# One gate unit moved from the state-space stage to the second attention, and a wait on copies put behind the products that don't read them

## The reference, cut to what matters

```python
proj = h @ w_in                      # the last 3 * 1024 columns are gate_logits
o_mla = causal_block_attention(q_mla, k_mla, v_mla)
o_fox = causal_block_attention(q_fox, k_fox, v_fox, cum_log_f)
o_s5 = s5_branch(u, ...)
gates = sigmoid(gate_logits.reshape(bsz, seq, 3, 1024))
merged = einsum('bsnd,bsnd->bsd', gates, projected)
x = x + merged @ w_out
x = x + conv_gated_ffn(rms_norm(x), ...)
```

## Time and profile before

| what | value |
|---|---|
| median of 3 runs | 1455.21 us (1454.87 to 1455.35) |
| the profiled execution: its own time | 1453.84 us |
| its span, first to last instruction | 1451.8 us |
| mean granted clock of PE, as a share of full speed | 0.998 |
| PE busy | 1430.5 us (99%), 7067 matmuls |
| DVE / ACT / POOL busy | 985.6 / 664.0 / 157.7 us |
| fox attention, about | 170 to 327 us |
| second attention, its first scores to its last values | 377.4 to 528.2 us |
| state-space stage up to its output products | 532.5 to 630.4 us |

### The profile page before, as it was taken

The page is one execution under the profiler, slowest core; times in us unless marked ns, Lnnn a source line. Parts: engine busy times, 40 slices in busy tenths (PEclk is TensorE's granted clock), DMA queues, the critical chain, the costliest instruction groups (busy, mean ns, idle before and its releaser), DMA issues.

```text
span 1451.8 us, 19018 instructions
## 1 busy us (share of the span) xinstructions
PE 1430.5 (99%) x7067; PEld 1203.3 (83%) x7067; DVE 985.6 (68%) x1430; ACT 664.0 (46%) x1074; POOL 157.7 (11%) x163
## 2 busy tenths in 40 slices
PE   8999999999999999999999999999999999999998
PEld 6999988888788888887888888888888888888887
DVE  5213556656866557839927688877778786678886
ACT  6231455645445542136513455555555555544332
POOL 1001620112361112013201000000000000000000
PEclk9999999999999999999999999999999999999999
DMA  7202021140121133337552222222222222990222
GB/s 267 63 0 95 26 73 45 51 160 28 46 60 52 37 88 95 75 127 245 187 219 70 88 73 88 87 87 73 75 86 87 88 87 84 325 388 30 94 73 80
DMA packets 130406, 148.94 MB, mean 103 GB/s; under 512 B 11338, under 2 KB 95229, under 8 KB 130045
## 3 DMA queue, kind: packets, MB, share of 16 engines
q1 hardware_dynamic: 130128, 147.68, 30.8%
q10 hardware_dynamic: 189, 0.08, 0.0%
HBM read 110.83 MB, written 36.31 MB: 101 GB/s over the span
## 4 chain that ended last, share of the span: by engine, by line
PE 89%; DVE 4%; ACT 2%; DMA 2%; issue 1%; SPq 1%; POOL 1%; ACTq 0%; DVEq 0%
PE ps L2195 29%; PE ps L673 13%; PE ps L2502 5%; PE ps L2504 5%; PE ps L2503 5%; PE ps L2593 4%; PE ps L370 3%; PE ps L371 3%; PE ps L372 3%; PE ps L862 2%; PE ps L3075 2%; PE ps L3073 2%; PE ps L3074 2%; PE ps L841 2%; PE ps L1504 2%; DMA scr_gate<-plain_arena 1%
## 5 line engine op out<-in xcount | busy, mean ns | idle before, releaser
L2195 PE MATMUL ps<-split_arena 128*128 128x512 f32 x1320 | 306.8, 390 | 0.0
L673 PE MATMUL ps<-split_arena 128*128 128x512 f32 x1152 | 291.1, 400 | 2.1 <-ACT plain_arena L708 2.1
L2195 PEld LDWEIGHTS ps<-split_arena 128*128 128x128 f32 x1320 | 247.6, 188 | 51.4 <-issue 0.3
L673 PEld LDWEIGHTS ps<-split_arena 128*128 128x128 f32 x1152 | 209.1, 189 | 42.8 <-issue 3.6
L2378 ACT ACTIVATE down_ops<-down_all 128x1024 fp32r<-128x1024 f32 x77 | 81.6, 1061 | 115.5 <-PE ps L2504 115.4
L2195 PE MATMUL ps<-up_b,split_arena 128*128 128x512 f32 x528 | 126.5, 389 | 0.0
L2397 DVE TENSOR_TENSOR down_ops<-down_all,down_ops 128x1024 fp32r<-128x1024 f32 x77 | 94.0, 1222 | 46.4 <-ACT down_ops L2378 46.3
L2502 PE MATMUL ps<-down_ops 128*128 128x512 f32 x308 | 120.0, 390 | 0.5 <-DVE down_ops L2397 0.5
L2503 PE MATMUL ps<-down_ops 128*128 128x512 f32 x308 | 120.0, 389 | 0.0
L2504 PE MATMUL ps<-down_ops 128*128 128x512 f32 x308 | 119.9, 389 | 0.0
L2195 PEld LDWEIGHTS ps<-up_b,split_arena 128*128 128x128 f32 x528 | 99.2, 188 | 20.5
(11 more groups left out here) (406 smaller groups left out, 2465.1 us busy)
## 6 DMA issues: line engine op xcount, KB each, us to landing
plain_arena<-in_w_in SPq DMA_DIRECT2D x24, 512.0 KB, 4.2
scr_gate<-plain_arena SPq DMA_DIRECT2D x48, 256.0 KB, 2.0
plain_arena<-scr_gate SPq DMA_DIRECT2D x24, 512.0 KB, 4.6
plain_arena<-in_w_up SPq DMA_DIRECT2D x22, 512.0 KB, 5.3
up_raw<-in_w_up SPq DMA_DIRECT2D x22, 512.0 KB, 4.9
scr_act<-plain_arena SPq DMA_DIRECT2D x22, 512.0 KB, 2.6
down_all<-scr_act SPq DMA_DIRECT2D x18, 512.0 KB, 9.4
down_all<-in_w_down SPq DMA_DIRECT2D x18, 512.0 KB, 10.2
```

What stands on the lines that cost most here:

```text
L673: mm = nc.tensor.matmul(m.ps[:, self.banks[half], :], w[:, k, :], src[:, k, h * BANK:(h + 1) * BANK], start=(j == 0), stop=(j == self.PER_ ...
L2195: mm = nc.tensor.matmul(o, self.w[j][w][:, k, :], self.h[j][k][h], start=(j in self.OPENS and k == 0 and n == 0), stop=(k == self.HK - 1 a ...
```

## The change

The number of units in the second attention goes from 6 to 7 and that of the s5 stage from 8 to 7; in the s5 stage 8 halves rather than 9 stand before the turning of w, so each of the stage's two long fills is 24 matmuls shorter. `MLA_FILL` takes the 48 matmuls: 24 more in head 0, 12 more in head 1, 12 more in head 2, none in head 3. Inside the heads they also change places. The second edit moves PE's wait for the copies of the turned w from ahead of the taps' products to behind them. SP's program text is not touched; its loops follow the constants.

```diff
--- before.py
+++ after.py
@@ -721,8 +721,8 @@
 
 
 
-FOX_FIRST, FOX_ATT, MLA_FIRST, MLA_PREP, MLA_ATT, S5_UNITS = 1, 6, 1, 2, 6, 8
-S5_FIRST_HALVES = 9
+FOX_FIRST, FOX_ATT, MLA_FIRST, MLA_PREP, MLA_ATT, S5_UNITS = 1, 6, 1, 2, 7, 7
+S5_FIRST_HALVES = 8
 FOX_UNITS = FOX_FIRST + FOX_ATT
 MLA_UNITS = MLA_FIRST + MLA_PREP + MLA_ATT
 assert FOX_UNITS + MLA_UNITS + S5_UNITS == 3 * KD
@@ -734,7 +734,9 @@
 LATER_HEAD = [(0, 8), (0, 8), (2, 6), (0, 7), (0, 6), (0, 4), (7, 6), (8, 10)]
 LAST_HEAD = [(0, 8), (0, 8), (2, 6), (0, 6), (0, 6), (0, 4), (8, 4), (12, 8)]
 FOX_FILL = [(14, 9), (4, 11), (2, 10), (0, 12), (0, 12), (0, 6), (6, 6), (8, 10)] + LATER_HEAD * (H - 2) + LAST_HEAD
-MLA_FILL = [(12, 8), (8, 4), (2, 10), (0, 8), (0, 6), (0, 4), (6, 6), (10, 8)] + LATER_HEAD * (H - 2) + LAST_HEAD
+MLA_FILL = ([(12, 8), (18, 6), (4, 8), (0, 12), (0, 8), (0, 8), (8, 6), (8, 10)]
+            + [(0, 8), (0, 8), (2, 6), (0, 8), (0, 8), (0, 8), (12, 4), (8, 12)]
+            + [(0, 6), (0, 6), (2, 8), (0, 7), (0, 7), (0, 8), (10, 6), (10, 14)] + LAST_HEAD)
 MLA_BEFORE = UNIT // 2
 MLA_BEHIND = (MLA_PREP + MLA_ATT) * UNIT - MLA_BEFORE - OPENING[0] - sum(map(sum, MLA_FILL))
 assert OPENING[1] + sum(map(sum, FOX_FILL)) == FOX_UNITS * UNIT
@@ -1784,7 +1786,6 @@
                 tr.then_inc(s["w_ps"], 1)
         pe.wait_ge(s["u_cp"], 4)
         pe.wait_ge(s["b_rdy"], 1)
-        pe.wait_ge(s["w_cp"], 4)
         pe.wait_ge(fill.out, 2 * (FOX_UNITS + MLA_UNITS) + S5_FIRST_HALVES)
 
         for g in range(GR):
@@ -1795,6 +1796,7 @@
             if g % 4 == 3:
                 mm.then_inc(s["k_ps"], 1)
 
+        pe.wait_ge(s["w_cp"], 4)
         for i in range(2):
             for j in range(J):
                 for g2 in range(2):
```

## The result

| | before | after |
|---|---|---|
| median of the runs | 1455.04 us (1453.78 to 1456.14, 6 runs) | 1460.53 us (1458.45 to 1462.45, 6 runs) |
| ratio | | 1.004, 95% interval 1.003 to 1.005 |
| profiled execution, span | 1453.84, 1451.8 us | 1462.45, 1460.3 us |
| mean granted clock of PE | 0.998 | 0.994 |

The changed kernel is slower by 5.5 us; 4.1 were forecast. The spans of the two profiled executions differ by 8.5 us, because this execution of the changed kernel came to the second attention late: its first score starts at 380.13 us, before at 377.37, through longer waits and a lower granted clock (0.91 against 0.96) in the first 40 us, which the change doesn't touch. To hold its times against rows of before, 2.76 us have to be taken off.

A forecast was written before the change was run, and what follows sets the result against it. PE's total work, busy 1430.5 of 1451.8 us, was taken as the bound, so only its idle and slow time could move. Head 0 +5.1, heads 1 and 2 -0.8, s5 -0.2 gave +4.1: 1459.3 us against the median, range 1456.5 to 1462.8.

The forecast's parts named there:

- The pause in head 0: Step 4: ACT's copy of unit 10's second half waits for the first half's late store; PE idles some 8.5 us.
- From there to the fill behind step 6: Head 0 after the pause: 9.9 us of work and waits plus 1.7 for the slow clock, reaching that fill at 423.2.
- the bound with the longer low clock: Head 0 if the clock stayed low twice as long after the pause: +6.8 us instead of +5.1.
- Heads 1 and 2: 12 more fills in each cover step 5's waits, less new waits in head 1: -0.8 us, between -1.3 and 0.
- The new one at the boundary: Head 1, between steps 5 and 6: PE waits 0.75 us for ACT's copy of a half before the next starts.
- State-space stage: s5 stage up to the output products: -1.35 + 1.1 - 0.8 + 0.8 = -0.2 us, between -0.9 and +0.6.
- The moved wait: s5 stage: the taps' products follow the turning of w at 1.66 us, not 3.01: -1.35 us, no cost in its new place.
- Unit 22's low part: Second long fill of s5: PE reaches unit 22 at 597.3, POOL's low part is ready at 598.4: new wait, +1.1 us.
- The next boundary: Second long fill, one half after unit 22: the store stands behind unit 23's load: 0.3 to 1.4 us, say +0.8.
- the case of no change: Rival: the pause comes but the clock doesn't fall, or DMAs land early: +2.4 us, 1457.6 us; chance 0.18.
- the slower one: Rival: clock low longer after the pause, or w late and the 0.75 us wait longer: +7.4, 1462.6 us; chance 0.2.
- The faster one: Rival: the store doesn't hold the copy ahead of step 5's exponential; head 0 gains 5.6 us, total 1448.6 us; chance 0.07.

The follow-up runs named there:

- e1: After with SP's 35 small loads issued in three groups behind the stores of units 10, 11 and 12, not all ahead of unit 10's: 1451.33 us, ratio 0.9985 to before.
- e2: After with only the last 8 of the 32 small loads put behind the stores of unit 10: 1455.71 us, ratio 1.001 to before.
- e3: After with the wait for the copies of w back ahead of the taps' products, so only the unit is moved: 1460.81 us, ratio 1.0046 to before.
- e4: Before with only the wait for the copies of the turned w moved behind the taps' products: 1452.95 us, ratio 0.9992 to before.
- e13: e8 with 8 fill matmuls moved from head 1's end into head 0, plus e12's two POOL edits: 1451.01 us, ratio 0.9978 to before.
- e8: e1 with ACT making unit 22's high part ahead of the copies of w and the sines: 1450.49 us, ratio 0.9972 to before.
- e12: e1 with POOL making unit 12's low part ahead of head 2's work and getting heads 2 and 3's tables in step 6: 1450.76 us, ratio 0.9973 to before.

## Why the prediction was right, point by point

**The pause in head 0: right.** Forecast for the copy 410.8 and for PE 411.55, measured 414.15 and 414.89, less 2.76 that is 411.39 and 412.13. PE was ready at 402.8 (forecast 403). The 0.6 us are SP's: the store went out at 406.66 in this count, 0.36 later than in before, and landed after 4.6 us instead of 4.4. e1 and e2 show that the loads ahead of it are the cause, by removing and by thinning them.

**From there to the fill behind step 6: the work right, the clock too low by 0.7.** Measured 427.25 - 414.89 = 12.36 us. At half clock PE worked from 414.89 to about 419.75, 4.9 us, which loses 2.4; the rest is 9.9 us, exactly the figure that was taken. The step that failed is "its price I take from the one fall that I see, 1.7 us": in before 3.4 us of work were slow, here 4.9. Head 0 in all: +6.4 measured, +5.1 forecast, and the bound with the longer low clock, +6.8, held it. The 2 us that the prediction takes from the Trainium skill (DMA: Bandwidth & Descriptors, anatomy of one DMA) are given there for DMAs issued by GpSimd, and without the time of the bytes. In this trace the gate's stores, issued by SP, land after 2.0 us in the median, and this one took 4.6.

**Heads 1 and 2: -0.8 forecast, -0.1 measured.** The old waits did go: 444.68, and two more in before,

```profile
447.04 0.64 PE L827 MATMUL ps<-ident,plain_arena 128*96 128x128 f32 x4 [0.30 <-DVE mla_pt L1016]
...
479.91 0.44 PE L818 MATMUL ps<-ident,plain_arena 128*128 128x128 f32 x2 [0.19 <-DVE split_arena L1013]
```

together 1.5 us with 0.25 for each stop. (I had taken 1.7 for two waits in each head; head 2 has one.) The new one at the boundary costs 461.45 - 460.51 - 0.13 = 0.8, as forecast (0.75). The one forecast for step 7, 0.15, did not come. In its place one at the end of step 6, which the forecast did not have, costs 466.46 - 465.09 - 0.91 = 0.46: it waits for DVE, not for a copy. That makes -0.2, and -0.1 is measured. The term was too hopeful by 0.7; with head 0's 1.3 it is why the sum fell short.

**State-space stage: -0.2 forecast, -0.4 measured** (from its first instruction on PE to the output products 97.88 us in before and 86.51 in after, of which the 48 fills are 10.97). The moved wait: the products start 1.75 us behind the turning, not 3.01, so -1.26 (forecast -1.35), and e3 and e4 give 1.0 and 1.4. Unit 22's low part: 618.25 - 606.32 - 10.97 = +0.96 (forecast 1.1). The next boundary: 624.33 - 618.25 - 5.48 = +0.6 (forecast 0.8), and the old one, 604.91 - 593.15 - 10.97 = 0.8, is gone as forecast. That DVE's end is hidden held with 1.4 us to spare. Against before DVE lost 0.6 us, less than the 1 to 1.5 allowed for: POOL's passes cost the scans 2.0 and the product on L1950 0.7 us, but in before a pass had cost the product on L1965 2.1 (3.29 us, where its neighbours take 1.22).

**The rivals.** The clock did fall, so the case of no change is out; the slower one came in part: with the later store and the longer low clock head 0 went 1.3 of the 1.7 us towards it. The faster one's condition, the store landing in time, was made true in e1, and its price was wrong: -5.6 for head 0 became -1.9. It took it that the waits behind DVE in steps 5 and 6 would go when PE had more fill. They grew by 1.7 us in their brackets, since faster fill moved POOL's pass onto DVE's division. That accounts for 3.0 us (3.4 from start to start, less the 0.4 that the rival had left there) of the 3.7 that are missing. The other 0.7 us stand in steps 1 to 3: from the first score to the fill behind step 4 e1 takes 402.95 - 377.45 = 25.50 us with 16 fills (3.66) more, before 24.96, a gain of 3.1 where the rival had 2.1 + 1.7 = 3.8. What holds PE there no run tells.

## What to carry to other kernels

When filler work gets faster, follow its by-products to their queue: each finished piece needs a copy, a store and a landing, and a store that is harmlessly late behind a row of small loads becomes the bound as soon as the next piece arrives before it lands. Put small loads that nobody needs soon behind the stores, and look at what each instruction ahead of a store waits for itself (e13). Where VectorE is on the path, look for the GpSimd instruction that starts just before each of its long rows, and ask where your change will put it.

## What the runs showed of the hardware that was not expected

- **The clock's fall is not the same from one execution to the next.** Behind an idle stretch of some 1.9 us at one place of head 0 the clock was low for 3.4 us in before and for 6.8 us in e4. Behind 1.98 us in e1 it didn't fall, and behind 1.96 us at the same place in e8, whose PE program up to there is the same, it did: the eight matmuls behind it took 2.10 us in e1 (its row at 410.38 above, at 2.4 GHz) and 3.52 in e8, for the most part at 1.2 GHz. The row is e8's:

```profile
410.82 3.52 PE L673 MATMUL ps<-split_arena 128*128 128x512 f32 x8
```

  In e12 1.66 us of idling were enough for a fall. In these five executions a stop of 1.7 to 2 us cost 0 to 3.4 us for the clock on top of itself, so one profiled execution doesn't give the price.
- **A load of 4 KB costs SP 0.46 us of its queue** (16 in 7.36 us), and everything that stands behind it in SP's program waits. The 256 KB store landed 4.4 us (before) and 4.6 us (after) after its issue, a 512 KB load having been issued 0.47 us before it; the median of these stores is 2.0 us.
- **GpSimd can hold a VectorE instruction of 0.29 us for 2.1 us.** Not every one is hit: in e1's s5 stage POOL's pass runs from 604.91 for 2.39 us, and the product on L1954, which reads PSUM, takes its usual 1.22 us from 605.23 on, while the one on L1955 behind it, with both inputs from SBUF, takes 1.89.
